# The sums of down weight blocks: from GpSimd in SBUF to DMAs in DRAM

## The reference

```python
xn = rms_norm(h, norm_mix_g)
proj = xn @ w_in                       # q, k, v of two attention mixers, 4608 columns
att_a, att_b = ...                     # chunked attention, 16 heads each
gates = jax.nn.sigmoid(xn @ w_gate)
merged = gates[..., :D] * (att_a @ w_branch_a) + gates[..., D:] * (att_b @ w_branch_b)
h = h + merged @ w_out
hn = rms_norm(h, norm_mlp_g)
u = jnp.square(jax.nn.relu(hn @ w_mlp_in))     # 2048 -> 8192
h = h + u @ w_mlp_out                          # 8192 -> 2048
return rms_norm(h, norm_final_g)
```

## Time and profile before

| what | us |
|---|---|
| median of 2 runs | 2721.8 (2721.12 to 2722.47) |
| the profiled execution, its own time | 2723.25 |
| its span, first to last instruction | 2721.5 |
| PE busy | 2560.5 |
| DVE busy | 1713.7 |
| POOL busy | 1023.0 |
| ACT busy | 976.9 |

### The profile page before, as it was taken

One profiled execution on the slowest core, in us unless ns is written; L12 is line 12 of the kernel. 1 busy time (PEld: TensorE's weight loads), 2 busy tenths in 40 slices (PEclk: granted clock), 3 DMA queues, 4 the chain that ended last, 5 costly groups with the idle time before them and its releaser, 6 DMA issues.

```text
span 2721.5 us, 34691 instructions
## 1 busy us (share of the span) xinstructions
PE 2560.5 (94%) x14354; PEld 2219.9 (82%) x14354; DVE 1713.7 (63%) x1894; ACT 976.9 (36%) x1246; POOL 1023.0 (38%) x560
## 2 busy tenths in 40 slices
PE   9999999999999999997999999999789888989886
PEld 8898888888888888887999999999777666767665
DVE  5565555455333334345666665666798999899888
ACT  4445443344222223123433333333343334333434
POOL 0000000000000000017777777777756577565743
PEclk9999999999999999998999999999899999999988
DMA  7222222222323334222443334333523332322221
GB/s 246 84 88 80 92 80 88 89 82 85 101 92 100 92 100 155 94 84 70 127 129 124 125 120 137 119 124 123 224 78 140 117 131 78 139 93 113 104 85 70
DMA packets 158064, 299.49 MB, mean 110 GB/s; under 512 B 8512, under 2 KB 113104, under 8 KB 149088
## 3 DMA queue, kind: packets, MB, share of 16 engines
q1 hardware_dynamic: 157776, 297.44, 32.5%
q10 hardware_dynamic: 144, 0.02, 0.0%
HBM read 276.41 MB, written 21.01 MB: 109 GB/s over the span
## 4 chain that ended last, share of the span: by engine, by line
PE 60%; DVE 22%; issue 7%; POOL 5%; ACT 3%; DMA 1%; SPq 0%; DVEq 0%; ACTq 0%; POOLq 0%
PE bank L1473 20%; PE bank L1475 19%; PE bank L1474 19%; DVE ring L1282 8%; DVE up_lo L1214 4%; POOL down_raw L1376 4%; DVE stream L1307 2%; ACT up_hi L782 2%; DVE down_forms L1273 2%; DVE hidden_out L1237 1%; PE bank L1579 1%; ACT ring L834 1%; PE bank L1562 1%; POOL up_raw L1376 1%; DMA up_raw<-in_up_units 1%
## 5 line engine op out<-in xcount | busy, mean ns | idle before, releaser
L1376 POOL TENSOR_TENSOR up_raw<-up_raw 128x256 f32<-128x256 f32 (+1 forms) x384 | 515.1, 1345 | 194.6 <-DMA up_raw<-in_up_units 173.9
L901 DVE TENSOR_TENSOR w_lo<-landing,w_hi 128x1024 fp32r<-128x1024 f32 x200 | 248.8, 1244 | 467.4 <-ACT w_hi L593 467.2
L1376 POOL TENSOR_TENSOR down_raw<-down_raw 128x1024 f32<-128x1024 f32 x128 | 385.7, 3031 | 265.6 <-DVE ring L1282 265.6
L1282 DVE TENSOR_TENSOR ring<-down_raw,ring 128x1024 fp32r<-128x1024 f32 x224 | 439.0, 1974 | 67.3 <-ACT ring L834 66.1
L1214 DVE TENSOR_TENSOR up_lo<-up_raw,up_hi 128x1792 fp32r<-128x1792 f32 x128 | 301.3, 2354 | 244.2 <-ACT up_hi L782 244.2
L1379 POOL TENSOR_TENSOR form_raw_a<-form_raw_a 128x1024 f32<-128x1024 f32 x3 | 8.1, 2730 | 1184.9 <-DVE form_raw_a L1185 1184.9
L593 ACT ACTIVATE w_hi<-landing 128x1024 fp32r<-128x1024 f32 x200 | 212.0, 1060 | 667.5 <-PE bank L1475 663.5
L834 ACT ACTIVATE ring<-down_raw 128x1024 fp32r<-128x1024 f32 x224 | 234.0, 1058 | 464.6 <-PE bank L1475 247.6
L782 ACT ACTIVATE up_hi<-up_raw 128x1792 fp32r<-128x1792 f32 x128 | 218.0, 1703 | 437.9 <-PE bank L1475 401.7
L1473 PE MATMUL bank<-xn_hi,w_hi 128*128 128x512 f32 x928 | 367.1, 396 | 2.8 <-DVE w_lo L901 2.2
L1475 PE MATMUL bank<-xn_hi,w_lo 128*128 128x512 f32 x928 | 361.8, 390 | 0.0
(11 more groups left out here) (167 smaller groups left out, 5257.9 us busy)
## 6 DMA issues: line engine op xcount, KB each, us to landing
up_raw<-in_up_units SPq DMA_DIRECT2D x128, 512.0 KB, 3.6
down_raw<-in_down_blocks SPq DMA_DIRECT2D x64, 1024.0 KB, 6.8
landing<-in_w_in SPq DMA_DIRECT2D x72, 512.0 KB, 3.6
landing<-in_w_gate SPq DMA_DIRECT2D x64, 512.0 KB, 3.7
landing<-in_w_out SPq DMA_DIRECT2D x32, 512.0 KB, 3.6
hidden_rows<-hidden_out SPq DMA_DIRECT2D x32, 512.0 KB, 5.3
raw_forms<-hidden_rows SPq DMA_DIRECT2D x17, 512.0 KB, 10.2
landing<-in_w_branch_a SPq DMA_DIRECT2D x16, 512.0 KB, 3.4
```

The source lines that it names most:

```text
L901: nc.vector.tensor_tensor(w_lo[:, s, :], landing[:, u % LAND, :], w_hi[:, s, :].bitcast(F32), ALU.subtract).then_inc(unit_lo, 1)
L1282: nc.vector.tensor_tensor(part[:, 1, :], raw, part[:, 0, :].bitcast(F32), ALU.subtract)\
L1376: return nc.gpsimd.tensor_tensor(out, a, b, ALU.add)
```

## The change

The sums of weight blocks are no longer made in the down stage. GpSimd's queue issues them as DMAs from DRAM to DRAM during the first stages, into a new DRAM tensor `down_totals`: a plain copy of one block, and then an accumulating DMA that adds another block to it. Each step m has four copies and four additions of 1 MB, in six rounds that wait for each other, and the set of step m starts when `unit_used` reaches 12 + 11m. They stand in GpSimd's order of work ahead of `form_sums` and `up_sums`. In the down stage SP loads every piece by itself, 0.5 MB, from `down_blocks` or `down_totals`, into one of 12 raw slots that together take the place of the six before; the load of piece i waits for the split of piece i - 12. GpSimd's `down_sum` goes, its forms of hidden tokens stay. The loads of the next chunk's hidden blocks are issued behind piece 2 of each odd step, and SP waits for all the totals once, before the first down load.

```diff
-RING, RAW_SLOTS, FORM_SLOTS = 4, 6, 10
+RING, RAW_SLOTS, FORM_SLOTS = 4, 12, 10
-PIECE_BLOCK = (0, 0, 0, 3, 1, 2, 0)
+BLOCK_OF, SUM_OF = {0: 0, 3: 3, 5: 2}, {1: 0, 4: 1, 2: 2, 6: 3}
...
+    down_totals = nc.dram_tensor("down_totals", (CHUNKS, 2, 4, P, 4, QC), F32, kind="Internal").ap()
...
-            def load_raw(w):
-
-                m, b = w // 4, w % 4
-                sp.dma_start(raw_of(w), down_blocks[m // 2, m % 2, b]).then_inc(down_landed[w % RAW_SLOTS], 16)
+            def load_raw(i):
+
+                m, j, h = i // PIECES, i % PIECES // 2, i % 2
+                src = down_blocks[m // 2, m % 2, BLOCK_OF[j]] if j in BLOCK_OF else down_totals[m // 2, m % 2, SUM_OF[j]]
+                sp.dma_start(down_raw[i % RAW_SLOTS], src[:, 2 * h:2 * h + 2, :]).then_inc(down_landed[i % RAW_SLOTS], 16)
...
             sp.wait_ge(up_lo_done, UP_UNITS - 1)
+            sp.wait_ge(totals_added, 16 * 4 * STEPS)
             load_raw(0)
+            load_raw(1)
...
+            sp.wait_ge(up_lo_done, UP_UNITS)
+            load_raw(2)
+            load_raw(3)
             load_hidden(0, 1, raw_form[places[0][3]])
-            sp.wait_ge(up_lo_done, UP_UNITS)
-            load_raw(1)
             store_hidden(SUBS - 2)
             sp.wait_ge(up_used, UP_UNITS)
-            load_raw(2)
-            load_raw(3)
+            for i in range(4, RAW_SLOTS):
+                load_raw(i)
+            store_hidden(SUBS - 1)
...
+            for i in range(RAW_SLOTS, PIECES * STEPS):
+                m, p = i // PIECES, i % PIECES
+                sp.wait_ge(piece_lo, i - RAW_SLOTS + 1)
+                load_raw(i)
+                if m % 2 == 1 and m < STEPS - 1 and p == 2:
                     c = m // 2 + 1
...
+            def totals(m):
+
+                blocks, sums = down_blocks[m // 2, m % 2], down_totals[m // 2, m % 2]
+
+                def copied(src, dst):
+                    pool.dma_start(dst, src).then_inc(totals_copied, 16)
+
+                def added(src, dst):
+                    pool.dma_start(dst, src, accum_op=ALU.add, max_dma_last_dim=8192).then_inc(totals_added, 16)
+
+                copied(blocks[0], sums[0])
+                copied(blocks[1], sums[1])
+                pool.wait_ge(totals_copied, 16 * (4 * m + 2))
+                added(blocks[1], sums[0])
+                added(blocks[2], sums[1])
+                pool.wait_ge(totals_added, 16 * (4 * m + 2))
+                copied(sums[0], sums[2])
+                pool.wait_ge(totals_copied, 16 * (4 * m + 3))
+                added(blocks[2], sums[2])
+                pool.wait_ge(totals_added, 16 * (4 * m + 3))
+                copied(sums[2], sums[3])
+                pool.wait_ge(totals_copied, 16 * (4 * m + 4))
+                added(blocks[3], sums[3])
+
+            for m in range(STEPS):
+                pool.wait_ge(unit_used, 12 + 11 * m)
+                totals(m)
             form_sums(form_raw_a, 0, 4, 8, 0)
...
             for m in range(STEPS):
-                landed(4 * m)
-                landed(4 * m + 1)
-                down_sum(m, 0, 1, 1, 0)
-                down_sum(m, 0, 1, 2, 1)
...
+                for products, f in enumerate((1, 2, 5, 4)):
+                    next_sum(m, f, products + 1)
```

More of the change, by code:

```diff
@@ L261, in build @@
         form_lo = [(form_lo_a, form_lo_b)[k // 4][:, k % 4, 0:FORMS] for k in range(KP)]
-        down_raw = [down_raw01[:, 0], down_raw01[:, 1], down_raw2[:], down_raw3[:], down_raw45[:, 0], down_raw45[:, 1]]
+        down_raw = [down_raw01[:, k // 2, k % 2 * 2:k % 2 * 2 + 2] for k in range(4)]
+        down_raw += [down_raw2[:, 0:2], down_raw2[:, 2:4], down_raw3[:, 0:2], down_raw3[:, 2:4]]
+        down_raw += [down_raw45[:, k // 2, k % 2 * 2:k % 2 * 2 + 2] for k in range(4)]
         ring = [ring0[:], ring12[:, 0], ring12[:, 1], ring3[:]]
@@ L371, in build @@
         down_landed = [sem(f"down_landed{k}") for k in range(RAW_SLOTS)]
-        down_summed = sem("down_summed")
+        totals_copied = sem("totals_copied")
+        totals_added = sem("totals_added")
         piece_hi = sem("piece_hi")
@@ L414, in down_bank, with raw_of @@
             return (((6, 0)[m % 2]), 2, 4, (6, 0)[m % 2], 4, 2, 4)[j]
-        def raw_of(w):
-            return down_raw[w % RAW_SLOTS]
+        def raw_of(i):
+            return down_raw[i % RAW_SLOTS].rearrange("p k n -> p (k n)")
         block = ctx.enter_context(nc.Block())
@@ L570, in _ @@
                         sp.wait_ge(piece_used, PIECES * 2 * (c - 1))
+                    load_hidden(c, 3, raw_form[places[c][6]])
                     load_hidden(c, 0, raw_form[places[c][0]])
-                    load_hidden(c, 3, raw_form[places[c][6]])
                     load_hidden(c, 1, raw_form[places[c][3]])
[L574 to L577, removed]
             for t in range(TT):
@@ L820, in piece_high @@
             def piece_high(i):
[L822 to L827, removed]
+                act.wait_ge(down_landed[i % RAW_SLOTS], 16 * (i // RAW_SLOTS) + 16)
                 if i == 0:
@@ L833, in piece_high @@
                     act.wait_ge(piece_used, i - RING + 1)
-                nc.scalar.activation(ring[i % RING][:, 0, :], raw_of(w)[:, 2 * h:2 * h + 2, :].rearrange("p k n -> p (k n)"),
-                                     ACT.Copy).then_inc(piece_hi, 1)
+                nc.scalar.activation(ring[i % RING][:, 0, :], raw_of(i), ACT.Copy).then_inc(piece_hi, 1)
             def final_squares(q, t, k):
@@ L1276, in piece_low @@
             def piece_low(i):
[L1278 removed]
                 dve.wait_ge(piece_hi, i + 1)
                 part = ring[i % RING]
[L1281 to L1282 removed]
+                nc.vector.tensor_tensor(part[:, 1, :], raw_of(i), part[:, 0, :].bitcast(F32), ALU.subtract)\
                     .then_inc(piece_lo, 1)
@@ L1436, in next_sum @@
                     block_sum(m // 2 + 1, f)
[L1438 to L1446, removed]
             for f in (1, 2, 5, 4):
```

12 lines of the change are left out of this document (removed).

## The result

The changed kernel takes 2580.2 us (median of 2 runs, 2579.65 to 2580.73) against 2721.8 before: a ratio of 0.9478, 95% interval 0.9451 to 0.9506. The prediction said 2600, range 2574 to 2780. The profiled execution took 2580.73 us with a span of 2578.9.

What follows compares the result with a forecast made beforehand. TensorE was taken as the bound, held in the down stage by VectorE, which GpSimd's sums slow. 2723.3 - 125 (down stage) + 3 (first stages) = 2601, with the median 1.4 below the profiled execution: 2600 us, range 2574 to 2780.

Steps and rivals of the forecast that it cites:

- T: GpSimd's DMA queue in the first stages: time of one step's eight DMAs in six rounds, put at 59.4 us.
- floor of 609.3 us: Down stage: 2688 matmuls at 0.2267 us each, TensorE's time there if it never waits.
- 36.5 us of stalls: Down stage: stalls expected to remain of the 161.5 us above pure matmul time, leaving a gain of 125 us.
- my bound of 151: Down stage: most us to be won, with 10 us of stalls left, if the ring hides all of the odd steps.
- The 17.5 us for odd steps: Down stage: 2.5 us of stall charged for each of the 7 odd steps before the last.
- hidden sums at 2.2 us each: Odd down steps: four GpSimd sums of hidden forms cost VectorE up to 8.8 us, making 45.0 against TensorE's 38.1.
- Loads of the stage at no cost: Down stage: 224 loads of 0.5 MB replace 64 of 1 MB at cost zero, covered by 30 us between issue and need.
- my 62.4: Before the up stage: largest time in us of one step's DMA set at which the form sums are still on time.
- The deadline: Before the up stage: GpSimd's form sums must not be held past 1197 us, or TensorE pays nearly the whole delay.
- First stages at +3: First stages: weight unit loads sharing engines with the DRAM sums still fit; 3 us charged for the whole.
- Rival 2: First stages: each of a set's eight DMAs waits for a VectorE instruction; set 69.2 us, delay 61, time 2661; chance 0.10.
- Rival 3: Down stage: odd steps pay all their 6.9 us or more; 81 us won, time 2644 us; chance 0.12.

## Why the prediction was right

The step that carried it held: GpSimd's sums, and for the greater part not their place in a chain, cost VectorE its time (sums left out: 2572.2; sums put back with nobody waiting: 2691.8). The number is 20 us off: 25.6 us too many stalls in the down stage and 5.1 too few in the first stages, of opposite sign. And there was luck in T: its terms were rows of SP's loads, since none showed a DMA of GpSimd, and nothing in them promised that it would come out within 3 us. Point by point:

- **The floor and the gain of the down stage.** The floor of 609.3 us held. I left 36.5 us of stalls, measured are 10.9; gain 150.6 instead of 125, almost my bound of 151. All 10.9 lie in the first 21.3 us, against the 8 us that I gave step 0: TensorE isn't busy for 7.8 us there, and the rest is the clock of 0.76. The 17.5 us for odd steps, the 8 for steps 14 and 15 and the 3 for the end were nothing.
- **The mis-sized term: hidden sums at 2.2 us each, and so 45.0 us of VectorE in an odd step.** Measured in VectorE's own order, from the first piece of an odd step to the first of the next (steps 3, 5 and so on to 13): 35 instructions with 39.7 us of durations, which cover 37.6 us of time as neighbours overlap slightly, just within TensorE's 38.1. (The 34.2 of the window above leaves out some of them.) VectorE takes 41.9 us from start to start of an odd step and 34.3 of an even one, TensorE 38.1 for each without a pause, so the ring did hide the unevenness, as I had hoped for part of it. The sums' whole price is what the means lie above the medians: 224 x (1285 - 1216) + 40 x (1490 - 1212) + 16 x (1436 - 1213) ns = 30 us for 32 sums, 0.9 us each (1490 and 1436 are the means of the two groups of form halves). I had priced each by its worst meeting, 1.23 against 3.37 us in the earlier trace rows; most meetings are cheaper: the 29 ring pieces that meet one have a mean of 1.74 us, 0.5 above one alone. Four sums at 0.9 in place of 2.2 us are 5 of the 5.3 us between 45.0 and 39.7. Corrections came down to 0.746 us, as said, and the ring mean to 1285 ns (1.3).
- **Loads of the stage at no cost.** Right: ScalarE waited 1.7 us for them, with a share of 0.61 (0.57 said).
- **T.** 59.4 us said, 56.5 measured: copies 6.1 (from totals) and 7.1 (from blocks) against 6.8, additions 9.5 against 9.9. The second read was in the sum at 3.1 us and costs 2.2. By the rule of the Trainium skill (Collectives: The Full Stack, "Why ReduceScatter is half of AllGather"), which is given there for rings between ranks, an add reads twice and moves half as much; here it is 30% on 7.3 us, so the direction agrees and the size doesn't.
- **Lateness.** Not late, as said, but by an argument that was too strict: GpSimd doesn't wait for a set's last addition, only SP does, at the first down load. What holds GpSimd is 47.2 us in the first set (124.64 + 0.82 - 78.29) and 47.4 on average, not T, against gates 59.7 us apart. So T could have been some 9.5 us (one landing) above my 62.4 before the form sums were late. The deadline itself was right within about 1 us (with late sets 48.4 us of delay for 49.5).
- **First stages at +3.** Measured +8.1, of which 6.5 are one late unit. I had averaged DMA shares; what hurt was one meeting of 4 MB of x with set 14. That the stall needs the set is shown: without sets, with sets elsewhere and with shorter ones it is gone, and with another part of a set there it is 0.81 us. That the loads of x are the other half rests on their times in the trace, and wasn't tried by itself. The rest, 1.6 us, arises in the up stage. From its first matmul to the first down matmul it takes 690.3 us before and 691.8 here, but 688.5 when the same changed kernel was profiled again and 691.8 in the kernel without DMAs (688.5 to 692.4 over all the kernels profiled). So the 1.6 us lie within the scatter of that stage.
- **Rival 2, descriptors behind VectorE.** Its T of 69.2 us isn't there (56.5). The issue takes a median of 0.52 us for a copy (0.68 at most) and 0.84 for an addition (1.19 at most), with VectorE busy 33 to 56% around it. The box in the Trainium skill (SBUF — State Buffer, "SBUF: two separate sides") speaks of VectorE work that holds both ports; no sign of such a wait is in this trace. **Rival 3, VectorE as the limit**, fell, but only by the 0.5 us between 37.6 and 38.1 in an odd step, and by the ring.

## What to carry to other kernels

Where a two-input VectorE instruction is the limit, look at what GpSimd does beside it before looking at VectorE's own list; work that depends only on weights can go to DMAs in a stage whose DMA engines are two thirds idle, as the first stages were here. Price a collision by how often it happens (mean less median over the group), not by its worst pair. And when DMAs are moved into a quiet stage, look for the single burst that is already there, and for what the issuing engine really waits for: the issue or the landing.

## What the hardware showed

- A stall of TensorE of 3.44 us in an otherwise full stage was followed by 5.7 us of matmuls at 0.63 us in place of 0.39, at a granted clock of 0.50: the price of one late load (6.5 us) was nearly twice its wait. A stall of 0.81 us at the same place, in the kernel with later sets, was followed by matmuls at 0.39 us.
- GpSimd reading SBUF slows a two-input VectorE instruction; GpSimd only writing doesn't (102 pieces at a mean of 1.22 us).
- Accumulating in DRAM costs 9.5 us for 1 MB beside other loads, against 7.3 for a copy of the same descriptors. VectorE and ScalarE don't feel it (their splits of weight units have the same means as before, 1244 and 1060 ns), but the unit loads of 0.5 MB beside it land in medians of 4.7 to 5.7 us, where they were 3.4 to 3.7.
